# Folding a norm's gain into the first mixer's weights, and cutting the first loads, the first row tile and the first product into pieces

## The reference, cut to what matters

```python
def rms_norm(x, g):
    y = x32 * lax.rsqrt(jnp.mean(x32 * x32, axis=-1, keepdims=True) + EPS)
    return (y * g.astype(jnp.float32)).astype(x.dtype)
...
u = rms_norm(h, norm_mix[0])
z = u @ w_in                      # 1024 x 3584: q, f, inp, g, gate_b, gate_c, h_b
forget = lb + (1.0 - lb) * jax.nn.sigmoid(f)   # lb: cumsum of softmax(hgrn_lb_logits)
```

## Time and profile before

| what | value |
|---|---|
| median of 3 runs | 1201.29 us (1199.64 to 1202.44) |
| profiled execution, its time / its span | 1200.2 us / 1198.1 us |
| PE, DVE, ACT, POOL busy | 1156.7, 893.2, 741.9, 137.3 us |
| DMA | 287.58 MB, mean 240 GB/s |

### The profile page before, as it was taken

How to read it: one execution, slowest core, us unless ns; L and a number is a source line. 1 busy time by engine, 2 the same in 40 slices (tenths; PEclk the granted TensorE clock), 3 DMA queues, 4 the chain that set the end, 5 groups by cost and what they waited for, 6 DMA issues and landing times.

```text
span 1198.1 us, 16842 instructions
## 1 busy us (share of the span) xinstructions
PE 1156.7 (97%) x5770; PEld 927.1 (77%) x5770; DVE 893.2 (75%) x1164; ACT 741.9 (62%) x910; POOL 137.3 (11%) x100
## 2 busy tenths in 40 slices
PE   5999999999999999999999999998999999999996
PEld 4778888786788888888778885685788888888775
DVE  6642346826799999999886449836799999999875
ACT  5553220233777887887756439733788788788654
POOL 0000000000121221221100000001022122121100
PEclk9999999999999999999999999998999999999998
DMA  9573211142599999999692220233699999999631
GB/s 381 186 301 106 71 36 71 36 176 106 203 361 383 381 381 378 372 381 381 251 354 86 91 86 2 92 119 114 230 351 393 377 377 385 377 376 387 258 137 70
DMA packets 50084, 287.58 MB, mean 240 GB/s; under 512 B 9215, under 2 KB 9215, under 8 KB 20720
## 3 DMA queue, kind: packets, MB, share of 16 engines
q1 hardware_dynamic: 34256, 243.06, 53.3%
q0 software_dynamic: 15776, 43.82, 9.8%
HBM read 272.68 MB, written 30.41 MB: 253 GB/s over the span
## 4 chain that ended last, share of the span: by engine, by line
PE 85%; DVE 7%; ACT 3%; DMA 3%; issue 2%; SPq 0%; POOLq 0%; DVEq 0%; ACTq 0%
PE psum L471 80%; PE psum L773 2%; DVE arena L2274 2%; ACT whi L1137 1%; DMA arena<-vscr,cur 1%; DVE arena L2287 1%; PE psum L814 1%; DMA raw<-w_dense_dram 1%; PE psum L538 1%; DVE wlo L1657 1%; PE psum L702 1%; ACT ahi L1137 0%; DVE alo L1713 0%; DMA arena<-yscr 0%; ACT arena L1137 0%
## 5 line engine op out<-in xcount | busy, mean ns | idle before, releaser
L1657 DVE TENSOR_TENSOR wlo<-raw,whi 128x2048 fp32r<-128x2048 f32 x213 | 485.7, 2289 | 99.1 <-ACT whi L1137 86.8
L471 PE MATMUL psum<-whi,ahi 128*128 128x512 f32 (+1 forms) x1184 | 470.4, 397 | 9.9 <-issue 3.8
L471 PE MATMUL psum<-whi,alo 128*128 128x512 f32 (+1 forms) x1184 | 459.5, 388 | 0.0
L471 PE MATMUL psum<-wlo,ahi 128*128 128x512 f32 (+1 forms) x1184 | 458.4, 387 | 0.0
L1137 ACT ACTIVATE whi<-raw 128x2048 fp32r<-128x2048 f32 (+1 forms) x215 | 409.6, 1907 | 77.0 <-PE psum L471 73.6
L471 PEld LDWEIGHTS psum<-whi,ahi 128*128 128x128 f32 x1184 | 222.9, 188 | 57.7 <-issue 7.8
L471 PEld LDWEIGHTS psum<-whi,alo 128*128 128x128 f32 x1184 | 222.7, 188 | 47.2
L471 PEld LDWEIGHTS psum<-wlo,ahi 128*128 128x128 f32 x1184 | 223.3, 189 | 41.0
L1137 ACT ACTIVATE arena<-psum 128x512 f32<-128x512 f32 (+1 forms) x141 | 80.9, 584 | 145.6 <-PE psum L471 117.6
L1137 ACT ACTIVATE ahi<-psum 128x512 fp32r<-128x512 f32 x146 | 81.7, 593 | 82.4 <-PE psum L773 35.7
L471 PE MATMUL psum<-arena 128*128 128x512 f32 (+9 forms) x802 | 128.3, 332 | 4.5 <-DVE arena L2000 4.4
(11 more groups left out here) (188 smaller groups left out, 860.7 us busy)
## 6 DMA issues: line engine op xcount, KB each, us to landing
raw<-w_moe_dram SPq DMA_DIRECT2D x192, 1024.0 KB, 8.9
raw<-w_dense_dram SPq DMA_DIRECT2D x35, 1024.0 KB, 7.7
yscr<-arena POOLq DMA_DIRECT2D x2, 4096.0 KB, 23.6
arena<-yscr POOLq DMA_DIRECT2D x8, 1024.0 KB, 7.0
vscr<-arena POOLq DMA_DIRECT2D x8, 512.0 KB, 2.9
arena<-w_proj_dram POOLq DMA_DIRECT2D x2, 1024.0 KB, 6.6
arena<-gains_dram POOLq DMA_DIRECT2D x3, 512.0 KB, 3.8
out_dram<-arena SPq DMA_DIRECT2D x3, 512.0 KB, 2.6
```

The source lines that it names most:

```text
L471: return nc.tensor.matmul(o, l, r, start=start, stop=stop, **kw)
L1657: tt(wlo[:, b % SPL, :], raw[:, b % RAW, :], halves(whi[:, b % SPL, :]), ALU.subtract).then_inc(lo_ready, 1)
```

## The change

It has these parts:

- The gain of the first norm is no longer multiplied into the rows. It comes as a 128 x 8 column block behind the constants (`AR_GMIX0`) and is multiplied into chunks 0 to 13 while they are split (`folded`, b < 14). The 512 KB load of gain rows goes; `xn` of norm 0 is one TENSOR_SCALAR multiply by 1/rms.
- SP issues row tile 0 first, then the constants, the 8 gain columns (4 KB), chunk 0 in two halves with a semaphore each, and then the rest as before.
- Row tile 0: ACT sums the squares of columns 0 to 511, DVE those of 512 to 1023, and `xn` is written in two halves.
- Chunk 0 is split in four pieces, in both ACT and DVE, and PE's first group (`first_tile`) takes its twelve matmuls in the order in which the pieces come.
- The first transposes alternate between banks 4, 5 and 6, 7 (`first_bank`), so that a tile's transposes need not wait for the tile just before.
- PE runs products whose result nobody reads: 40 of 128 x 128 bf16 before the first transposes, 10 before and 10 behind the first group.
- Tile 2's transposes stand behind group (0,1), tile 3's in the middle of group (0,2). Chunk 1 is split on ACT and DVE behind all four row tiles.

```diff
+            if b < 14:
+                return [(slice(t * 512, t * 512 + 512), gmix0(b % 2 * 4 + t)) for t in range(4)]
...
-            sp.dma_start(con[:, :], consts).then_inc(s_con, 16)
...
             rows_in(0)
-            sp.dma_start(area(AR_GAIN, D), gains[0]).then_inc(s_gain0, 16)
-            load(0, w_dense[0])
+            sp.dma_start(con[:, :], consts[:, 0:CONST_N]).then_inc(s_con, 16)
+            sp.dma_start(area(AR_GMIX0, KT), consts[:, CONST_N:CONST_N + KT])\
+                .then_inc(s_gmix0, 16)
+            sp.dma_start(raw[:, 0, 0:D], w_dense[0][:, 0:D]).then_inc(w0_full, 16)
+            sp.dma_start(raw[:, 0, D:], w_dense[0][:, D:]).then_inc(w_full[0], 16)
             rows_in(1)
...
             pe.wait_ge(s_con, 16)
-            norm_T(0, 0)
+            first_T(0)
+            unread(WARM // 4)
+            first_tile()
+            unread(WARM // 4)
+            first_T(1)
+            def wait_first(i, q):
+                pe.wait_ge(n_lo, first_lo(q, i))
+            def third_T(i, q):
+                if i == 0 and q == 1:
+                    first_T(2)
+            def fourth_T(i, q):
+                if i == 0 and q == 2:
+                    first_T(3)
...
-            dense(BLK["f"], "act", before=wait_norm(0), after=first_T, first=w0_lo)
+            dense(BLK["f"], "act", before=wait_first, after=third_T, mid=fourth_T, order=TILES[1:])
...
             act.wait_ge(w_full[0], 16)
-            copy(whi[:, 0, 0:D], raw[:, 0, 0:D]).then_inc(w0_hi, 1)
-            norm_hi(0, 0)
-            copy(whi[:, 0, D:], raw[:, 0, D:]).then_inc(hi_ready, 1)
+            first_w(2)
+            first_w(3)
             todo[0] = 1
-            for tb in range(1, TB):
-                root(0, tb)
-            norm_hi(0, 1)
-            splits(2)
-            for tb in range(2, TB):
-                norm_hi(0, tb)
+            act.wait_ge(s_con, 16)
+            root(0, 1)
+            first_hi(0, 1)
+            first_hi(1, 0)
+            root(0, 2)
+            first_hi(1, 1)
+            square(0, 3)
+            first_hi(2, 0)
+            sqrt(0, 3)
+            first_hi(2, 1)
+            first_hi(3, 0)
+            first_hi(3, 1)
             splits(3)
...
             norm_x(0, 1)
+            first_split(1, 0)
+            first_split(0, 1)
             norm_x(0, 2)
-            norm_lo(0, 1)
+            first_split(1, 1)
+            first_split(2, 0)
             norm_x(0, 3)
-            norm_lo(0, 2)
-            splits(2)
-            norm_lo(0, 3)
+            first_split(2, 1)
+            first_split(3, 0)
+            first_split(3, 1)
             nc.vector.tensor_copy(upper, c_("upper"))
-            nc.vector.memset(ones, 1.0)
             splits(2)
```

More of the change, by code:

```diff
@@ L38 @@
 STEPS = PASSES * EXP
+WARM = 40
 FAR = 4096.0
@@ L96 @@
 AR_Y3 = 14848
+AR_GMIX0 = 14800
 ARENA = 15360
@@ L471, in mm, with dense @@
                 return nc.tensor.matmul(o, l, r, start=start, stop=stop, **kw)
-            def dense(k, lhs, tiles=(0, 4), before=None, after=None, order=TILES, first=None, mid=None):
+            def dense(k, lhs, tiles=(0, 4), before=None, after=None, order=TILES, mid=None):
                 for i, q in order:
@@ L480, in dense @@
                     if q == 0:
-                        if i == 0 and first:
-                            pe.wait_ge(first, 1)
-                        else:
-                            pe.wait_ge(lo_ready, c + 1)
+                        pe.wait_ge(lo_ready, c + 1)
                     if i == 0:
@@ L540, in norm_T, with unread, first_T, first_tile @@
                     last.then_inc(n_t, 1)
-            pe.wait_ge(s_con, 16)
-            norm_T(0, 0)
+            def unread(n):
+                for t in range(n):
+                    mm(PS[7][:, 0:P], ones, ones, True, True)
+            def first_T(tb):
+                for half in range(2):
+                    if tb == 0 and half == 0:
+                        pe.wait_ge(x0, 3)
+                    else:
+                        pe.wait_ge(n_xn, nrows(0, tb))
+                    if tb > 1:
+                        pe.wait_ge(n_lo, first_lo(tb - 2, half))
+                    for t in range(4):
+                        kt = half * 4 + t
+                        last = nc.tensor.transpose(first_bank(tb, half)[:, t * P:(t + 1) * P],
+                                                   xn(tb)[:, kt * P:(kt + 1) * P], ident)
+                    last.then_inc(n_t, 1)
+            def first_tile():
+                def hh(t):
+                    pe.wait_ge(*((w0_hi, t + 1) if t < 3 else (hi_ready, 1)))
+                    mm(PS[0][:, :], ahi[:, t, 0:P], whi[:, 0, t * 512:t * 512 + 512], t == 0, False)
+                def hl(t):
+                    pe.wait_ge(*((w0_lo, t + 1) if t < 3 else (lo_ready, 1)))
+                    mm(PS[0][:, :], ahi[:, t, 0:P], wlo[:, 0, t * 512:t * 512 + 512], False, False)
+                def lh(t):
+                    mm(PS[0][:, :], alo[:, t, 0:P], whi[:, 0, t * 512:t * 512 + 512], False, False)
+                pe.wait_ge(n_hi, 1)
+                hh(0)
+                hl(0)
+                hh(1)
+                pe.wait_ge(n_lo, first_lo(0, 0))
+                lh(0)
+                lh(1)
+                hh(2)
+                lh(2)
+                hl(1)
+                hh(3)
+                lh(3)
+                hl(2)
+                hl(3)
+            pe.wait_ge(x0, 1)
+            unread(WARM)
+            pe.wait_ge(s_con, 16)
+            first_T(0)
[11 more added lines that the diff above has]
+                    first_T(3)
             def wait_norm(n):
```

91 lines of the change are left out of this document (65 added, 26 removed).

## The result

The changed kernel takes 1209.22 us (median of 6, 1204.75 to 1210.27), the kernel before 1201.12 (6 runs, 1198.72 to 1202.44): ratio 1.0069, 95% interval 1.0057 to 1.0081, so 8.1 us slower. Slower was forecast, by 3.1, and 1209.22 lies above the range given (1200.0 to 1207.0). The profiled execution has a span of 1208.5 us against 1198.1, 10.4 more.

A forecast was written before the change was run, and what follows sets the result against it. PE bounds the kernel, let into the q block at 40.70 by DVE's lb chain and chunk 2 split. Later entry +1.9, clock fall +1.2, the rest nothing: 1201.29 + 3.1 = 1204.4 us, range 1200.0 to 1207.0.

The forecast's parts named there:

- The bound: At PE's entry into the q block (40.70), PE's f block and DVE's lb chain balance, DVE's later by 0.24 us.
- The landing of chunk 0's first half: At the start: lands at 7.37, as the gain rows with as many bytes ahead did.
- chain to q entry: DVE's lb chain begins at 27.75, takes 12.06 us, then chunk 2's split 2.74; PE enters the q block at 42.6.
- wait ahead of (1,0): PE waits 1.8 us for DVE's split of chunk 1 before group (1,0), the first to need chunk 1, starts at 27.85.
- (d): Rival at the front: landings later, say 2 us; lb chain 3.5 us later than before; +5.2, 1206.5. Half in 10.
- The loss at the q entry: PE's first product of the q block comes at 42.6 instead of 40.70: +1.9 us, bounds 1.4 to 2.6.
- The four-way split of chunks 1 and 2: Chunk 1 takes ACT 2.57 us for 1.9, DVE 2.74 for 2.2; chunk 2 takes 2.74 for 2.35.
- The clock: PE idles 3.85 us before the q block, its clock falls, 3.4 us of work at half rate: +1.2 (0.6 to 1.7).
- The rest: nothing: Pieces of chunks 3 to 13 cost nothing, since PE waits for neither DVE nor ACT; the freed 512 KB load likewise.
- (b): Rival: PE runs group (0,1) at the lower rate too, 4.48 us instead of 2.83; all behind 1.65 later, 1206.1. 1 in 10.
- (a): Rival at the q block: the same path, but the clock stays up: +1.9, 1203.2. 2 in 10.
- (c): Rival: DVE comes to the lb chain early, part of the gain is kept; 1197.5 if it never waited. 1.5 in 10.

The follow-up runs named there:

- c1_c2_early: Changed kernel with chunk 1 split earlier on ACT and DVE, and DVE's split of chunk 2 ahead of the lb chain: 1202.18 us, ratio 1.0020.
- early_cold: early_all without the unread products (`WARM = 0`): 1198.36 us, ratio 0.9987 to the kernel before.
- cold_nofold: after_cold with chunks 1 to 13 split whole and the first mixer's norm vector left out, so layer 0 routes otherwise: 1204.09 us, ratio 1.0029.
- before_fold: Kernel before, with chunks 1 to 13 split in four scaled pieces on ACT and DVE: 1201.30 us, ratio 1.0014.
- after_cold: Changed kernel without its 60 unread products (`WARM = 0`): 1206.85 us, ratio 1.0054 to the kernel before.
- gains4: Changed kernel with the gains tensor in DRAM at its old size, so tensors behind it lie where they lay: 1209.15 us, ratio 1.0063.
- after_pad: Changed kernel with two redundant PE waits behind every three products of blocks q, v, g and C, 128 instructions more: 1205.97 us, ratio 1.0044.
- before_unread_pad: before_unread with two redundant PE waits behind every three products of blocks q, v, g and C: 1200.42 us, ratio 1.0006.
- before_waits: Kernel before, with 242 redundant waits ahead of PE's first transposes (120 instructions more in PE's stream), no product added: 1205.91 us, ratio 1.0044.
- early_all: c1_c2_early, with ACT's split of chunk 3 behind the four sigmoids of the f block: 1202.09 us, ratio 1.0014 to the kernel before.
- early_pad: early_all with the redundant PE waits of after_pad: 1198.12 us, ratio 0.9988 to the kernel before.
- before_unread: Kernel before, with 40 unread products ahead of PE's first transposes and 10 behind them: 1200.35 us, ratio 1.0016, runs from 1196.60 to 1212.35.
- a_again: The changed kernel, unchanged, measured and profiled once more: 1208.02 us, ratio 1.0067 to the kernel before.
- c1_early: Changed kernel with chunk 1 split earlier: on ACT ahead of row tile 3, on DVE between its halves: 1208.66 us, ratio 1.0067.
- before_late: Kernel before, with nine more TENSOR_SCALARs on DVE ahead of the lb chain, to delay it: 1207.66 us, ratio 1.0059.

## Why the prediction was right in sign and short in size

**The bound.** It was read rightly: two paths in balance at 40.70, and DVE's lb chain decides. c1_c2_early shows it by taking chunk 2 out from behind the chain: 3.3 of the 3.85 us go, and with ACT's chunk 3 moved too the front's gain is kept (38.25 in early_cold).

**The landing of chunk 0's first half** is the first term that was mis-sized. I took 7.37, the landing of as many bytes in the kernel before; it landed at 8.82, 1.45 later. It carries through: (0,1) at 16.34 for 14.8, row tile 3's transposes at 22.77 for 20.9, DVE's chunk 1 at 26.97 for 25.1, the lb chain at 29.63 for 27.75, q entry 44.55 for 42.6. Of the 1.95 us at the q entry the other 0.5 was lost in the steps between. The durations behind were right: chain to q entry 14.92 (14.85 forecast), wait ahead of (1,0) 1.86 (1.8). Why these bytes landed later than the gain rows had, no run takes apart. My bounds for this term allowed +0.7; later landings were rival (d), at half in 10.

**The loss at the q entry**, +1.9, was +3.85. The four-way split of chunks 1 and 2 is 1.5 of it, in cold_nofold and in before_fold alike, and my terms for it were right (0.67 on ACT, 0.54 on DVE, 0.39 for chunk 2). The other 2.4 is chunk 1 behind row tile 3, with a row tile 3 that came 1.9 later than I had it.

**The clock**, +1.2, was in truth one of two prices. In the changed kernel, its repeat and after_cold it falls behind the 1.86 us ahead of (1,0) already, at a place where I expected none; the f block then ends at 42.5, where it ends at 41.1 in gains4 without that fall, inside DVE's delay, and only 0.44 us are left behind the entry (191.14 for 190.70). In gains4 and after_pad it stays up there, PE idles 3.6 us at the entry, and the fall behind it costs 3.0 to 3.2 (193.70 and 193.88), above my upper bound of 1.7: the low clock did not end with 3.4 us of work (0.50 over all of 45 to 50). My reading of the earlier trace rows was slightly off besides: 0.59 in the half microsecond from 292.5 puts the end of that fall at 292.9, not 292.7. The same program goes either way; both sum to more than my +3.1, namely 4.3 and, in after_pad, 6.8.

**"The rest: nothing"** was the step that failed in kind: the sum has no term for anything behind 230 us. Up to the MoE that holds. In layer 0's MoE 6.0 us come in the profile: 3.0 more of waiting (3.29 for 0.28) for a gather that lands after 10.6 us instead of 7.6, and the rest by the clock that falls behind that wait. I had costed the unread products by their time on PE alone, nothing, and for PE alone that is right (before_unread_pad, 1.0006). What they do is to shift the fetches of PE's stream by 120 instructions. That the fetch's place decides is shown from both sides: put on the gather without products (before_waits) and taken off it with the products kept (after_pad, before_unread_pad).

**Rivals.** (b) fell: group (0,1) took 2.87 us, 16.34 to 19.21, the full rate, with ten unread products and eight transposes ahead of it; and in after_cold, with transposes alone, 2.86 (16.41 to 19.27). (a), no clock fall, fell: there was one in every profile of the changed kernel, gains4, after_pad and after_cold, only not always at the q entry. (d), later landings, came closest at the front: 1.45 of its 2 us, and +3.85 of its +5.2. (c) was the right mechanism for another kernel: chunk 1 split ahead of row tile 3's last half is what early_all does, and chunk 2 had to go ahead of the chain as well.

**The sum.** On medians the changed kernel and its repeat stand at 1.0069 and 1.0067, without the fetch on the gather at 1.0044 (after_pad) and 1.0054 (after_cold). So as an estimate 2 to 3 of the 8.1 us are the fetch and the rest the front, which agrees with the 4.3 and 6.8 of the profiles. The split is rough: each ratio is known to about 0.0015, some 2 us, and after_cold's interval overlaps the changed kernel's. It is clearer between early_all and early_pad, 1.0014 and 0.9988. In the seven profiles with a late landing the MoE stretch is 294.5 to 297.0 us, so 3.6 to 6.0 over before; that medians show less would fit a wait that comes in some runs only, as in before_unread. How often it comes in the changed kernel, and why c1_c2_early's profile escaped it, stays open. So does how one packet of 16 KB holds a few of the gather's packets back by 2 to 3 us: it was seen that it does, not where the two meet.

## What to carry to other kernels

Before a gain at the front is counted on, look for the next point where two paths are in balance, and ask what of the moved work stands ahead of the other path; a landing is to be priced by its own bytes and pieces, not by the load that stood in its place. Instructions that cost their engine nothing still shift everything fetched behind them: if a gather or another small transfer far away lands some us later after such a change, count the instructions added, look where the instruction queue's packets fall, and add as many as put them back (here 249 more than before, in after_pad). And a test whether a shift or a content does harm is cheap: delay the old kernel by the same amount.

## What was unexpected of the hardware

- A packet of the instruction queue 2 to 4 us behind the issue of a gather, under a full load of chunks, went with a landing after 10.2 to 10.8 us in five profiles and 7.9 in one, PE let go 9.9 and 10.2 after the issue in two where the view gives no landing. Where the packet was 11 us or more away it was 7.6 to 7.8 in all nine. Late are four to eight of the gather's 144 packets, those that start more than 8 us behind the issue; in the nine and in c1_c2_early's there is none.
- The granted clock fell behind 1.83 to 1.86 us of idling at (1,0) in three profiles (the changed kernel's, a_again's, after_cold's) and not behind 1.85 us at the same place in gains4 and after_pad. At the q entry it fell behind 3.60 to 4.24 us in four (gains4, after_pad, c1_early, before_late), and behind 2.54 in c1_c2_early, but not behind 3.12 in cold_nofold, which then ran at the full rate to 231 (190.74 us). So the length of the idle time alone does not tell. The way from the entry to the wait at 231 was 2.6 to 3.2 us longer in the four and 1.7 in c1_c2_early.
- Redundant waits in a row are slow on PE when it has nothing else: in before_waits' profile 120 wait instructions stand from 3.6 to 16.6 us, 0.11 apart. Among 512-column products 128 of them cost 0.2 us at most (193.88 for 193.70).
- Forty unread products ahead of the first eight transposes brought these to 1.06 or 1.07 us in five profiles (the changed kernel's, c1_early's, gains4's, after_pad's, early_all's) and left them at 1.94, as without any, in five others (a_again's, c1_c2_early's, early_pad's, before_unread's, before_unread_pad's). In c1_early and early_all the clock fell again within the first group (0.66 and 0.67 from 10 to 15).
- In the kernel before the granted clock reads 1.00 from 10 to 15, while the products of that stretch start 0.43 us apart, the low pace. At the very start of a profile the pace of the products is the better witness.
